# Where the token lists of the later experts come from: one-hot matmuls, or a table in DRAM

## The chip, the cores and the metric

The kernel runs on one core of a Trainium2 chip. The metric is the device time of one execution in microseconds (us); each figure is a median of runs. The core has TensorE (PE in the profile; PEld is its weight load), VectorE (DVE), ScalarE (ACT), GpSimd (POOL) and SyncE (SP), each with an instruction queue of its own, and 16 DMA engines. Engines wait for each other through semaphores only.

## The reference

One layer of a diffusion backbone over T = 384 tokens of width 1024. The first half (adaLN modulation, latent attention, a Conformer convolution) is not touched. The second half is a mixture of experts:

```
scores = sigmoid(t @ router_w)                      # (384, 64)
# 4 of 8 groups, then the best 8 of 64 experts per token; w = their scores, normalised, times 2.5
gates  = sum(one_hot(idx, 64) * w)                  # (384, 64), 8 entries per row are not zero
hid    = silu(t @ exp_w_gate[e]) * (t @ exp_w_up[e]) * gates[:, e]
routed = sum over e of hid @ exp_w_down[e]          # 64 experts, 3 MB of fp32 weights each
x      = x + gate2 * (routed + shared)              # then one final RMSNorm
```

## The kernel before

The instructions of each engine are written out by hand, in the order in which they run; nothing reorders them. After the router, the kernel takes one expert per **step** j: up to 128 tokens of expert j are gathered, sent through its three matrices and scattered. (An expert with over 128 tokens would need more rounds; the number of rounds is read from the data. In the run shown there is one round, 64 steps.) Steps 0 to 7 are unrolled, the middle ones are a hardware loop over blocks of 8 (`in_order`, L462), the last 8 and three to drain are unrolled again.

The **list** of an expert says, for each of 128 slots, which token sits there (`ixt[:, k, 0]`, the row of `h2_d` to gather), which row of `y_d` its result goes to (`ixt[:, k, 1]`, the token times 8 plus the rank of the expert among the token's 8) and with which gate (`gsl[:, k]`). `slot` is the partition that a position has. Before the change each list is made from `pos3` (each token's position in each expert's list, or a large number) and `vals` (token, destination, and the gate in two parts) in three moves:

- DVE `onehot` (L1537) compares `pos3` of one expert with `slot`: a 128x384 tensor of ones and zeros;
- PE `token_list` (L2060): three matmuls of that one-hot with the expert's 4 columns of `vals`, into bank 5;
- DVE `list_of` (L1547) turns the bank into integers `ixt` and the gate `gsl`, and counts up `list_done`.

What each engine does in step k, in order (numbers are experts):

- SP (L642) waits for a raw buffer to be used and loads gate and up weights of k+3, then down weights of k+1. Each load is 1 MB.
- ACT (L1113): silu of k-1, hidden of k-2 (`hidden_hi`), high part of the gate weights of k+1, `rows_out` of k-3 (PSUM to `ys`, two copies, L1110 and L1111), gathered tokens of k+1 (`turn_hi`), high part of the down weights of k-1 (L1078), high part of the up weights of k+1 (L1069).
- DVE (L1634): `hidden` of k-1 (L1599), `hidden_lo`, low part of the gate weights of k+1 (L1455), `list_of` of k+3, `onehot` of k+4, `turn_lo` of k+1 (L1590), low part of the down weights of k-1 (L1584), low part of the up weights of k+1 (L1455 again).
- PE (L2145): `token_list` of k+3, transposes of the tokens of k+1 (L1756), gate and up matmuls of k+1 (24 of 128x512), transposes of the hidden of k-1, then the down matmuls of k-2 (12). Each product is three matmuls (high x high, high x low, low x high), lines L1746 to L1748.
- POOL (L790): `gather` of k+3 (L776), which waits for `list_done`, then `scatter` of k-3 (L785). Both are indirect DMAs.

There are two `ys` buffers. So `rows_out` of k-3 waits until the scatter of k-5, issued two steps before, has landed (L1107).

Of the kernel before, what the change touches and what calls it, by code (L numbers as in the profile page):

```python
# [21 lines left out]
I32 = mybir.dt.int32  # L22
ALU = mybir.AluOpType
# [25 lines left out]
UNROLL = 8  # L49
NO_TOKEN = 4096  # L50


def constants():
# [84 lines left out]
def hybrid_step(nc, x_prompt, x_sample, cache_ckv, cache_krope, c, c_ctx, mod_w, mod_b, norm1_g, w_in,  # L138
# [11 lines left out]
    with ExitStack() as ctx:  # L150
# [124 lines left out]
        token_i = sb("token_i", [P, 1], A + 5.9375, I32)  # L275
        gsl = sb("gsl", [P, UNROLL], R + 8.375)
        sg = sb("sg", [P, FF], R + 9)
        hd = [sb(f"hd{i}", [P, FF], R + 10 + i) for i in range(2)]
# [19 lines left out]
        mod_d = dram("mod_d", [2, 4 * D])  # L298
        y_d = dram("y_d", [T * TOPK, D])

        def conv_slot(k):
# [17 lines left out]
        sinv = cst_of("sin").rearrange("p (t a f) -> p t a f", t=2, a=2)  # L319
        token = cst_of("token")  # L320
        V_G1, V_CB, V_LG, V_LB, V_QG, V_C = 0, 8, 16, 24, 32, 35

# [32 lines left out]
        mod_rows_out, g1_in, a2_in, b2_in = (sem(n) for n in ("mod_rows_out", "g1_in", "a2_in", "b2_in"))  # L355
        x1_done, ssq2_done, r2v, r2a, h2_done = (sem(n) for n in ("x1_done", "ssq2_done", "r2v", "r2a", "h2_done"))
        x1_out = sem("x1_out")
# [368 lines left out]
        def _(pool):  # L726
            pool.memset(zb[:, :, :], 0.0).then_inc(zeros_done, 1)

            pool.wait_ge(latn_done, 2 * NT)
# [50 lines left out]
            def scatter(i, k, last=False):  # L780
# [24 lines left out]
        def _(act):  # L805
# [221 lines left out]
            def mean_square2(t):  # L1027

                act.wait_ge(x1_done, NT + t + 1)
                act.activation(junk2[:, :], x1[:, t, :], ACT.Square, accum_out=stat[:, 40 + t:41 + t]).then_inc(ssq2_done, 1)  # L1030
                act.wait_ge(ssq2_done, t + 1)
                act.activation(stat[:, 44 + t:45 + t], stat[:, 40 + t:41 + t], ACT.Sqrt, scale=1.0 / D,
                               bias=stat[:, 53:54]).then_inc(r2a, 1)

# [132 lines left out]
            for t in range(NT):  # L1167
# [3 lines left out]
                act.activation(tjunk[:, :], acc[:, t, :], ACT.Square, accum_out=stat[:, 16 + t:17 + t]).then_inc(ssq2_done, 1)  # L1171
                act.wait_ge(r2v, t + 1)
                act.activation(stat[:, 60 + t:61 + t], stat[:, 57 + t:58 + t], ACT.Sqrt).then_inc(r2a, 1)


        @block.vector
        def _(dve):
# [254 lines left out]
            def normed2(t):  # L1432

                dve.wait_ge(r2a, t + 1)
                link(dve, "v", dve.reciprocal(stat[:, 48 + t:49 + t], stat[:, 44 + t:45 + t]))
# [111 lines left out]
            def list_of(i, k):  # L1547
                j = i * UNROLL + k
                if isinstance(j, int) and j < 2:
                    p = got(dve, ("list", j))  # L1550
                else:
# [42 lines left out]
            def hidden(i, k):  # L1594
                j = i * UNROLL + k
                dve.wait_ge(sg_done, j + 1)
                if from_step(j, 2):
# [3 lines left out]
                                         op0=ALU.mult, op1=ALU.mult).then_inc(hd_done, 1)  # L1601

            sums = {"all": 0}

# [29 lines left out]
            def step(i, k, left=99):  # L1634
# [31 lines left out]
            turn_lo(0, 0)  # L1666
            shared_hidden(2)
            in_order(dve, step)


# [30 lines left out]
            def normed(t):  # L1701

                dve.wait_ge(ssq2_done, NT + t + 1)
                dve.tensor_scalar(stat[:, 57 + t:58 + t], stat[:, 16 + t:17 + t], 1.0 / D, EPS, ALU.mult, ALU.add).then_inc(r2v, 1)
                dve.wait_ge(r2a, NT + t + 1)
                link(dve, "v", dve.reciprocal(stat[:, 60 + t:61 + t], stat[:, 60 + t:61 + t]))
# [23 lines left out]
        def _(pe):  # L1730
# [500 lines left out]
```

## Time and profile before

| | us |
|---|---|
| median of 3 runs | 1185.79 (1184.06 to 1187.43) |
| the profiled execution's own time | 1187.37 |
| its span, first to last instruction | 1185.6 |
| PE busy, share of the span | 1125.1, 95% |
| DVE busy | 1034.8, 87% |
| ACT busy | 796.4, 67% |
| POOL busy | 235.0, 20% |
| experts' steps | from about 516 to 1145 |

Lines L12 are lines of the kernel. PE's ends are modelled, so its busy share says little; the start of one matmul to the start of the next says more. An idle time is put down to the instruction or DMA that ended it. TensorE's granted clock was 0.98 of full speed over the span.

### The profile page before, as it was taken

The page shows a single profiled execution, that of the slowest core. Times are in us where ns is not written, and L with a number is a line of the kernel's source. Part 1 is how long each engine was busy: PE and PEld are TensorE (multiplying, and loading weights), DVE is VectorE, ACT ScalarE, POOL GpSimd, SP SyncE. Part 2 cuts the span into 40 slices and gives each one's busy share as a digit, 9 for nine tenths or more (in the row PEclk, how much of TensorE's full clock was granted, in tenths as well). Part 3 has the DMA queues.
Part 4 walks back from the last instruction along what each step waited for, and adds up shares of the span by engine and source line. Part 5 has one row for each costly group of instructions (what it writes and reads, how often), then busy time and mean ns, then how long its engine had stood idle before and what let it go on. Part 6 is the DMA issues. An engine that isn't in the chain of part 4 may idle for free.

```text
span 1185.6 us, 16767 instructions
## 1 busy us (share of the span) xinstructions
PE 1125.1 (95%) x5625; PEld 918.9 (78%) x5625; DVE 1034.8 (87%) x1382; ACT 796.4 (67%) x992; POOL 235.0 (20%) x182
## 2 busy tenths in 40 slices
PE   4999999998999999989999999999999999999984
PEld 1799999864557798658888888888888888888851
DVE  4769999989996565869998999999999999999977
ACT  6543232767873632748887888888888888888831
POOL 1000000001123001223422323332323323222210
PEclk8999999998999989999999999999999999999997
DMA  9673446635547227859999999999999999999994
GB/s 349 183 182 107 143 148 171 182 116 173 163 122 235 80 78 274 326 216 343 378 362 356 365 373 369 377 363 346 354 354 365 359 358 380 364 374 365 357 416 178
DMA packets 123259, 329.10 MB, mean 278 GB/s; under 512 B 28248, under 2 KB 69815, under 8 KB 98375
## 3 DMA queue, kind: packets, MB, share of 16 engines
q1 hardware_dynamic: 98656, 290.39, 66.8%
q0 software_dynamic: 21584, 33.79, 8.4%
q10 hardware_dynamic: 2968, 4.26, 1.0%
q8 instruction: 30, 0.49, 0.2%
q14 instruction: 21, 0.17, 0.0%
HBM read 327.70 MB, written 41.66 MB: 312 GB/s over the span
## 4 chain that ended last, share of the span: by engine, by line
PE 75%; DVE 9%; DMA 8%; ACT 5%; issue 2%; SPq 0%; POOL 0%; DVEq 0%; ACTq 0%; POOLq 0%
PE bank L1746 19%; PE bank L1748 19%; PE bank L1747 19%; PE bank L1756 7%; DMA raw<-in_exp_w_down_dram 3%; DVE lgu L1455 2%; DMA y_d<-ys,ixt 2%; PE bank L1941 2%; ACT hi L816 2%; PE bank L1929 1%; DVE lo L1584 1%; PE bank L1762 1%; DMA row1b<-y_d 1%; DMA raw<-in_mod_w_dram 1%; PE bank L1763 1%
## 5 line engine op out<-in xcount | busy, mean ns | idle before, releaser
L1455 DVE TENSOR_TENSOR lgu<-raw,hgu 128x2048 fp32r<-128x2048 f32 x128 | 292.0, 2282 | 1.3 <-ACT hgu L1069 1.3
L1069 ACT ACTIVATE hgu<-raw 128x2048 fp32r<-128x2048 f32 x128 | 245.4, 1917 | 0.4 <-DMA raw<-in_exp_w_gate_dram 0.4
L1746 PE MATMUL bank<-hgu,xgh 128*128 128x512 f32 x512 | 205.8, 402 | 2.4 <-DVE lgu L1455 2.1
L1748 PE MATMUL bank<-hgu,xgl 128*128 128x512 f32 x512 | 200.6, 392 | 0.0
L1747 PE MATMUL bank<-lgu,xgh 128*128 128x512 f32 x512 | 199.2, 389 | 0.0
L1584 DVE TENSOR_TENSOR lo<-raw,hi 128x2048 fp32r<-128x2048 f32 x64 | 147.7, 2308 | 27.8 <-ACT hi L1078 20.1
L1186 DVE TENSOR_TENSOR lo<-raw,hi 128x2048 fp32r<-128x2048 f32 (+2 forms) x57 | 125.8, 2209 | 29.9 <-ACT hi L816 29.9
L776 POOL DMA_INDIRECT xg<-h_d,ixt x64 | 66.3, 1036 | 399.1 <-DVE gsl L1557 372.5
L1078 ACT ACTIVATE hi<-raw 128x2048 fp32r<-128x2048 f32 x64 | 122.9, 1921 | 28.4 <-DMA raw<-in_exp_w_down_dram 28.4
L1284 DVE SCALAR_TENSOR_TENSOR zb<-zb,cwt 128x400 f32<-128x400 f32 x240 | 135.7, 634 | 0.6
L785 POOL DMA_INDIRECT y_d<-ys,ixt x62 | 124.7, 2011 | 48.3 <-ACT ys L1111 28.6
L816 ACT ACTIVATE hi<-raw 128x2048 fp32r<-128x2048 f32 (+2 forms) x57 | 105.1, 1846 | 18.8 <-PE bank L1748 16.0
L1746 PEld LDWEIGHTS bank<-hgu,xgh 128*128 128x128 f32 x512 | 96.2, 188 | 22.2 <-issue 3.2
L1748 PEld LDWEIGHTS bank<-hgu,xgl 128*128 128x128 f32 x512 | 96.1, 188 | 21.3
L1747 PEld LDWEIGHTS bank<-lgu,xgh 128*128 128x128 f32 x512 | 96.4, 188 | 18.5
L1746 PE MATMUL bank<-hi,hdh 128*128 128x512 f32 x256 | 106.4, 416 | 0.3 <-DVE hdl L1631 0.3
L1748 PE MATMUL bank<-hi,hdl 128*128 128x512 f32 x256 | 100.7, 393 | 0.0
L1747 PE MATMUL bank<-lo,hdh 128*128 128x512 f32 x256 | 99.5, 389 | 0.0
L1746 PE MATMUL bank<-hTh,hi 128*128 128x384 f32 x256 | 85.6, 334 | 0.0
L1748 PE MATMUL bank<-hTh,lo 128*128 128x384 f32 x256 | 85.5, 334 | 0.0
L1747 PE MATMUL bank<-hTl,hi 128*128 128x384 f32 x256 | 85.5, 334 | 0.0
L1590 DVE TENSOR_TENSOR xgl<-bank,xgh 128x512 fp32r<-128x512 f32 x128 | 82.0, 682 | 2.7 <-ACT xgh L1086 2.7
(306 smaller groups left out, 2081.0 us busy)
## 6 DMA issues: line engine op xcount, KB each, us to landing
raw<-in_exp_w_gate_dram SPq DMA_DIRECT2D x64, 1024.0 KB
raw<-in_exp_w_up_dram SPq DMA_DIRECT2D x64, 1024.0 KB
raw<-in_exp_w_down_dram SPq DMA_DIRECT2D x64, 1024.0 KB
raw<-in_mod_w_dram SPq DMA_DIRECT2D x20, 1024.0 KB, 5.2
raw<-in_w_in_dram SPq DMA_DIRECT2D x16, 512.0 KB, 5.4
raw<-in_w_in_dram SPq DMA_DIRECT2D x8, 1024.0 KB, 5.4
mraw<-in_mod_w_dram SPq DMA_DIRECT2D x4, 1024.0 KB, 15.7
raw<-in_w_o_attn_dram SPq DMA_DIRECT2D x4, 1024.0 KB, 5.0
```

Source lines behind the costliest of these rows:

```text
L785: pool.indirect_dma_start(y_d, bass.IndirectOffsetOnAxis(ap=ixt[:, k % UNROLL, 1:2], axis=0), (ys_last if last else ys)[k % 2][:, :], None ...
L816: act.activation(hi[place(i)][:, 0:k * w], tile[:, 0:k * w], ACT.Copy).then_inc(hi_done, 1)
L1069: act.activation(hgu[k % 2][:, :, w, :], src, ACT.Copy).then_inc(ghi_done, 1)
L1078: act.activation(hi[down_place(k, last)][:, :], raw[s][:, :], ACT.Copy).then_inc(dhi_done, 1)
L1186: dve.tensor_tensor(lo[place(i)][:, 0:k * w], tile[:, 0:k * w], hi[place(i)][:, 0:k * w].bitcast(F32), ALU.subtract).then_inc(lo_done, 1)
L1284: ins = dve.scalar_tensor_tensor(out=dst, in0=src, scalar=wk, in1=dst, op0=ALU.mult, op1=ALU.add)
L1455: dve.tensor_tensor(lgu[k % 2][:, :, w, :], src, hgu[k % 2][:, :, w, :].bitcast(F32), ALU.subtract).then_inc(glo_done, 1)
L1584: dve.tensor_tensor(lo[to][:, :], raw[s][:, :], hi[to][:, :].bitcast(F32), ALU.subtract).then_inc(dlo_done, 1)
L1746: pe.matmul(out, ah, bh, start=first, stop=False)
L1747: pe.matmul(out, ah, bl, start=False, stop=False)
L1748: return pe.matmul(out, al, bh, start=False, stop=last)
L1756: return pe.transpose(out, src, ident[0:n, 0:n])
```

## The change

Lists 0 to 10 are made as before. The others come from a table in DRAM, `lists_d`, with one row of four words (token, destination, gate, destination) for each of 128 slots of each expert:

- early, POOL fills the table with ones (as integers: an index out of bounds, which an indirect DMA leaves out);
- before step 0, DVE packs position and expert of each token's 8 choices in one key, sorts the keys with `max`, and unpacks them to the table row of each choice (`entry_rows`); in step 0 it picks the 8 gates of each token (`entry_gates`, 24 instructions);
- in steps 0 to 6 POOL writes the entries, 24 indirect DMAs of 128 rows of 16 bytes (`write_lists`); in step 7 it waits for them and reads the table into `listed`;
- from list 11 on, in steps 8 to 60, `token_list` on PE and `onehot` on DVE are gone, and `list_of` is two small copies out of `listed`; it stands at the end of DVE's step, behind the low part of the up weights, and not in its middle.

Two semaphores are merged with older ones (`r2v`, `r2a` with `rms_v`, `rms_a`), with the same order of events.

```diff
+KEY = 2048
+ON_TENSOR = UNROLL + 3
...
+    parts["key"] = np.broadcast_to(KEY * (NE - np.arange(NE))[None, :], (P, NE))
+    parts["dest"] = (TOPK * parts["token"][:, :, None] + np.arange(TOPK)).reshape(P, NT * TOPK)
...
 # gpsimd
             pool.memset(zb[:, :, :], 0.0).then_inc(zeros_done, 1)
+            pool.wait_ge(con_in, 16)
+            pool.dma_start(lists_d.rearrange("(q a) v -> q (a v)", q=P).rearrange("q (b n) -> q b n", n=P),
+                           ones.unsqueeze(1).to_broadcast([P, NJ * 4 // P, P])).then_inc(lists_out, 16)
...
+            def write_lists(first, end):
+                if first == 0:
+                    pool.wait_ge(lists_out, 16)
+                    pool.wait_ge(entry_done, 1)
+                for n in range(first, end):
+                    t, u = n // TOPK, n % TOPK
+                    pool.indirect_dma_start(lists_d, bass.IndirectOffsetOnAxis(ap=entry_row[:, t, u:u + 1], axis=0),
+                                            entry[:, t, u, :], None,
+                                            bounds_check=P * NJ - 1, oob_is_err=False).then_inc(lists_out, 16)
...
                 if from_step(j, 3):
                     scatter(i, k - 3, last=left <= -1)
+                if isinstance(j, int) and j < 7:
+                    write_lists(24 * j // 7, 24 * (j + 1) // 7)
+                if isinstance(j, int) and j == 7:
+                    pool.wait_ge(lists_out, 16 * (NT * TOPK + 1))
+                    pool.dma_start(listed[:, :, :], lists_d.rearrange("(q j) v -> q j v", q=P)).then_inc(lists_out, 16)
...
 # vector: list_of
+                if not isinstance(j, int) or j >= ON_TENSOR:
+                    dve.wait_ge(lists_out, 16 * (NT * TOPK + 2))
+                    dve.tensor_copy(ixt[:, k % UNROLL, :], listed[:, bass.ds(j, 1), 0:2].rearrange("p a v -> p (a v)").bitcast(I32))
+                    dve.tensor_copy(gsl[:, k % UNROLL:k % UNROLL + 1],
+                                    listed[:, bass.ds(j, 1), 2:3].rearrange("p a v -> p (a v)")).then_inc(list_done, 1)
+                    return
...
+            def entry_rows():   # 2 over 128x192, 3 max, then 10 of 128x24
...
+            def entry_gates():
+                for t in range(NT):
+                    for u in range(TOPK):
+                        ins = dve.scalar_tensor_tensor(out=key_gate[:, u, :], in0=keys[:, t, :], scalar=key8[:, t, u:u + 1],
+                                                       in1=rgate[:, t, :], op0=ALU.is_equal, op1=ALU.mult,
+                                                       accum_out=entry[:, t, u, 2:3])
...
+                ins.then_inc(entry_done, 1)
+                dve.wait_ge(entry_done, 1)
...
 # vector: step
-                if left > 3:
+                if isinstance(j, int) and j + 3 < ON_TENSOR:
                     list_of(i, k + 3)
-                if left > 4:
+                if isinstance(j, int) and j + 4 < ON_TENSOR:
                     onehot(i, k + 4)
                 if left > 1:
                     turn_lo(i, k + 1)
+                if isinstance(j, int) and j == 0:
+                    entry_gates()
...
                 if second:
                     down_lo(i, k - 1)
+                if left > 3 and not (isinstance(j, int) and j + 3 < ON_TENSOR):
+                    list_of(i, k + 3)
...
             shared_hidden(2)
+            entry_rows()
             in_order(dve, step)
...
 # tensor: step
-                if left > 3:
+                if isinstance(j, int) and j + 3 < ON_TENSOR:
                     token_list(i, k + 3)
```

On DVE, one step of the hardware loop before the change; `lgu` is the low part of gate or up weights, `lo` that of the down weights, `xgl` that of the gathered tokens, `oh` the one-hot:

```order
L1599 SCALAR_TENSOR_TENSOR hd_176<-bank,gsl,sg 128x256
L1631 TENSOR_TENSOR hdl_181<-bank,hdh_179 128x256
L1455 TENSOR_TENSOR lgu_160<-raw_49,hgu_158 128x8x256
L1556 TENSOR_SCALAR ixt<-bank 128x2
L1557 TENSOR_REDUCE gsl<-bank 128x1
L1544 TENSOR_TENSOR oh_171<-con,pos_129 128x384
L1590 TENSOR_TENSOR xgl_166<-bank,xgh_164 128x512
L1584 TENSOR_TENSOR lo_62<-raw_51,hi_59 128x2048
L1455 TENSOR_TENSOR lgu_160<-raw_50,hgu_158 128x8x256
```

The same step of the changed kernel, where `listed` is the table in SBUF:

```order
L1639 SCALAR_TENSOR_TENSOR hd_186<-bank,gsl,sg 128x256
L1707 TENSOR_TENSOR hdl_191<-bank,hdh_189 128x256
L1489 TENSOR_TENSOR lgu_160<-raw_49,hgu_158 128x8x256
L1630 TENSOR_TENSOR xgl_166<-bank,xgh_164 128x512
L1624 TENSOR_TENSOR lo_62<-raw_51,hi_59 128x2048
L1489 TENSOR_TENSOR lgu_160<-raw_50,hgu_158 128x8x256
L1592 COPY ixt<-listed 128x2
L1593 COPY gsl<-listed 128x1
L1639 SCALAR_TENSOR_TENSOR hd_187<-bank,gsl,sg 128x256
```

The one-hot is gone, and the pair that fills `ixt` and `gsl` has moved from the third place of the step to its end, past four large instructions. On POOL, steps 3 to 7 of the changed kernel, where `lists_d` is the table and `entry` what is written to it:

```order
L794 DMA xg0_162<-h2_d,ixt_172 128x1024
L803 DMA y_d<-ys0_168,ixt_172 3072x1024
L815 DMA lists_d<-entry_176,entry_row_177 24576x4 x3
L794 DMA xg1_163<-h2_d,ixt_172 128x1024
L803 DMA y_d<-ys1_169,ixt_172 3072x1024
L815 DMA lists_d<-entry_176,entry_row_177 24576x4 x4
L794 DMA xg0_162<-h2_d,ixt_172 128x1024
L803 DMA y_d<-ys0_168,ixt_172 3072x1024
L829 DMA listed_175<-lists_d 128x768
```

Three or four writes stand behind each scatter, and in the loop behind these rows gather and scatter alternate as before, the scatter always behind the gather of its step.

## Rows read from the trace of the kernel before

**Rows 1.** The page: busy us, share of the span, instructions.
```profile
PE 1125.1 (95%) x5625; PEld 918.9 (78%) x5625; DVE 1034.8 (87%) x1382; ACT 796.4 (67%) x992; POOL 235.0 (20%) x182
```
**Rows 2.** By stretch: PE, PEld, DVE, ACT, POOL busy us; PE clock, DMA share, GB/s.
```profile
740.00:780.00 40.00, 40.00 (x203) 33.81 (x202) 39.12 (x43) 34.65 (x37) 13.77 (x9) 1.00 0.96 378
...
860.00:900.00 40.00, 40.00 (x204) 33.78 (x203) 38.33 (x43) 34.30 (x38) 12.77 (x9) 1.00 0.94 354
```
**Rows 3.** The chain of work that ended last, 740 to 752: start us, us, what.
```profile
741.97 0.23 PE bank L2072 x3
742.20 0.95 PE bank L1756 x8
...
751.64 0.23 PE bank L2072 x3
```
**Rows 4.** All engines in time, one step: start us, us, what, [idle before].
```profile
742.01 0.60 ACT L1110 ACTIVATE ys<-bank 128x512 f32<-128x512 f32 x1 [0.42 <-PE bank L1748]
...
744.72 1.92 ACT L1078 ACTIVATE hi<-raw 128x2048 fp32r<-128x2048 f32 x1 [0.44 <-DMA raw<-in_exp_w_down_dram]
...
744.88 0.15 DVE L1557 TENSOR_REDUCE gsl<-bank 128x1 f32<-128x2 f32 x1
744.94 0.55 DVE L1544 TENSOR_TENSOR oh<-con,pos 128x384 fp32r<-128x384 f32 x1
...
745.84 1.01 POOL L776 DMA_INDIRECT xg<-h_d,ixt  x1 [5.20 <-DVE gsl L1557]
...
747.16 2.69 POOL L785 DMA_INDIRECT y_d<-ys,ixt  x1 [0.30 <-issue]
...
748.88 2.28 DVE L1455 TENSOR_TENSOR lgu<-raw,hgu 128x2048 fp32r<-128x2048 f32 x1
```
**Rows 5.** ACT in time, two steps later.
```profile
761.42 0.60 ACT L1110 ACTIVATE ys<-bank 128x512 f32<-128x512 f32 x1 [0.61 <-PE bank L1748]
```
**Rows 6.** Who waited for whom: us in total, times, longest us.
```profile
ACT hi L1078 <- DMA raw<-in_exp_w_down_dram: 28.4, 19, 4.0
...
ACT ys L1110 <- PE bank L1748: 26.4, 50, 0.9
```
**Rows 7.** Instructions of line L785, the scatters.
```profile
L785 POOL DMA_INDIRECT y_d<-ys,ixt x62: 961/1014/4836, 551.9 to 1138.4; - x62
...
DMA to landing us min/median/max: 7.0/7.1/7.2
```
**Rows 8.** Line L762, two early gathers of 128 rows.
```profile
DMA to landing us min/median/max: 10.1/10.5/11.0
```
**Rows 9.** The chain of work that ended last, 480 to 640.
```profile
561.09 15.30 DMA y_d<-ys,ixt
```
**Rows 10.** DVE in time, around steps 0 and 1.
```profile
522.70 0.16 DVE L1556 TENSOR_SCALAR ixt<-bank 128x2 int32<-128x2 f32 x1 [2.64 <-PE bank L2072]
...
527.34 0.48 DVE L1599 SCALAR_TENSOR_TENSOR hd<-bank,gsl,sg 128x256 f32<-128x256 f32 x1 [1.77 <-ACT sg L1094]
529.14 2.29 DVE L1455 TENSOR_TENSOR lgu<-raw,hgu 128x2048 fp32r<-128x2048 f32 x1 [1.31 <-ACT hgu L1069]
```
**Rows 11.** DVE in time, the router.
```profile
499.48 0.18 DVE L1496 TENSOR_SCALAR rgm<-rgm 128x24 f32<-128x24 f32 x1
...
500.08 0.48 DVE L1502 MAX8 rk<-rsel 128x8 f32<-128x64 f32 x3
...
506.23 0.89 DVE L1532 SCALAR_TENSOR_TENSOR pos<-bank,rtmp 128x192 f32<-128x192 f32 x3
```
**Rows 12.** The page: costliest groups: busy us, mean ns, idle before.
```profile
L785 POOL DMA_INDIRECT y_d<-ys,ixt x62 | 124.7, 2011 | 48.3 <-ACT ys L1111 28.6 <-issue 19.8
```
**Rows 13.** Who waited for whom, 505 to 605: us in total, times, longest.
```profile
POOL xg L776 <- DVE gsl L1557: 48.8, 8, 8.4
```
**Rows 14.** POOL in time, step 4.
```profile
559.78 1.01 POOL L776 DMA_INDIRECT xg<-h_d,ixt  x1 [3.01 <-DVE gsl L1557]
561.09 4.80 POOL L785 DMA_INDIRECT y_d<-ys,ixt  x1 [0.30 <-issue]
```

More of the change, by code:

```diff
@@ L276, in hybrid_step @@
         gsl = sb("gsl", [P, UNROLL], R + 8.375)
+        listed = sb("listed", [P, NJ, 4], R)
+        entry = sb("entry", [P, NT, TOPK, 4], A + 7.25)
+        entry_row = sb("entry_row", [P, NT, TOPK], A + 7.625, I32)
+        keys = sb("keys", [P, NT, NE], R + 14)
+        key_gate = sb("key_gate", [P, 8, NE], R + 12)
+        key8 = sb("key8", [P, NT, TOPK], R + 15)
+        key_i, key_p, key_q, key_r = (sb(f"key_{n}", [P, NT, TOPK], R + 15.125 + 0.125 * i, I32)
+                                      for i, n in enumerate("ipqr"))
         sg = sb("sg", [P, FF], R + 9)
@@ L355, in hybrid_step @@
         mod_rows_out, g1_in, a2_in, b2_in = (sem(n) for n in ("mod_rows_out", "g1_in", "a2_in", "b2_in"))
-        x1_done, ssq2_done, r2v, r2a, h2_done = (sem(n) for n in ("x1_done", "ssq2_done", "r2v", "r2a", "h2_done"))
+        x1_done, ssq2_done, h2_done = (sem(n) for n in ("x1_done", "ssq2_done", "h2_done"))
+        entry_done, lists_out = sem("entry_done"), sem("lists_out")
         x1_out = sem("x1_out")
@@ L1171, in _ @@
                 act.activation(tjunk[:, :], acc[:, t, :], ACT.Square, accum_out=stat[:, 16 + t:17 + t]).then_inc(ssq2_done, 1)
[L1172 to L1173 removed]
+                act.wait_ge(rms_v, t + 3)
+                act.activation(stat[:, 60 + t:61 + t], stat[:, 57 + t:58 + t], ACT.Sqrt).then_inc(rms_a, 1)
         @block.vector
@@ L1550, in list_of @@
                     p = got(dve, ("list", j))
-                else:
+                elif isinstance(j, int) and j < ON_TENSOR:
                     dve.wait_ge(list_filled, j - 1)
@@ L1601, in hidden @@
                                          op0=ALU.mult, op1=ALU.mult).then_inc(hd_done, 1)
+            def entry_rows():
+                first = pos3[:, :, 0:NE]
+                link(dve, "v", dve.scalar_tensor_tensor(out=keys[:, :, :], in0=first, scalar=512.0,
+                                                        in1=key_of.unsqueeze(1).to_broadcast([P, NT, NE]),
+                                                        op0=ALU.is_lt, op1=ALU.mult))
+                link(dve, "v", dve.tensor_tensor(keys[:, :, :], keys[:, :, :], first, ALU.add))
+                for t in range(NT):
+                    ins = dve.max(key8[:, t, :], keys[:, t, :])
+                dve.tensor_copy(entry[:, :, :, 0].bitcast(I32), token.unsqueeze(2).to_broadcast([P, NT, TOPK]))
+                for v in (1, 3):
+                    dve.tensor_copy(entry[:, :, :, v].bitcast(I32), dest)
+                link(dve, "v", ins)
+                link(dve, "v", dve.tensor_copy(key_i[:, :, :], key8[:, :, :]))
+                dve.tensor_scalar(key_p[:, :, :], key_i[:, :, :], 7, 4, ALU.bitwise_and, ALU.logical_shift_left)
+                dve.tensor_scalar(key_r[:, :, :], key_i[:, :, :], 1, NE * 3, ALU.logical_shift_right, ALU.bitwise_and)
+                link(dve, "v", dve.tensor_scalar(key_q[:, :, :], key_i[:, :, :], 3, 15, ALU.logical_shift_right, ALU.bitwise_and))
+                link(dve, "v", dve.tensor_tensor(key_p[:, :, :], key_p[:, :, :], key_q[:, :, :], ALU.add))
+                dve.tensor_scalar(key_q[:, :, :], key_i[:, :, :], 11, None, ALU.logical_shift_right)
+                link(dve, "v", dve.scalar_tensor_tensor(out=key_p[:, :, :], in0=key_p[:, :, :], scalar=float(NJ),
+                                                        in1=key_r[:, :, :], op0=ALU.mult, op1=ALU.add))
+                dve.scalar_tensor_tensor(out=entry_row[:, :, :], in0=key_p[:, :, :], scalar=float(NE),
+                                         in1=key_q[:, :, :], op0=ALU.add, op1=ALU.subtract)
@@ new lines, in entry_gates @@
+            def entry_gates():
+                for t in range(NT):
+                    for u in range(TOPK):
+                        ins = dve.scalar_tensor_tensor(out=key_gate[:, u, :], in0=keys[:, t, :], scalar=key8[:, t, u:u + 1],
+                                                       in1=rgate[:, t, :], op0=ALU.is_equal, op1=ALU.mult,
+                                                       accum_out=entry[:, t, u, 2:3])
+                    if t < NT - 1:
+                        link(dve, "v", ins)
+                ins.then_inc(entry_done, 1)
+                dve.wait_ge(entry_done, 1)
```

10 lines of the change are left out of this document (6 added, 4 removed).

## The prediction, made before the changed kernel was run

> **What bounds the kernel now.** I read the page's busy line first, then the experts' part by stretches, then the chain of waits inside one step, then who waits for whom. The page puts PE at 95% and DVE at 87% [rows 1], but these are means. In the experts' part PE is never idle, its clock is granted in full, DVE is busy for 38 to 39 of 40 us, ACT for 34, and the DMA engines for 0.94 to 0.96 of the time [rows 2]. So three resources are within a few per cent of each other, and a saving on one of them is worth only what the next one leaves.
>
> The chain inside a step is PE alone, with matmuls starting every 0.23 us. From one list's matmuls to the next list's it is 751.64 - 741.97 = 9.67 us [rows 3]; from one `rows_out` on ACT to that two steps later it is 761.42 - 742.01 = 19.41 us, 9.70 each [rows 4, 5]. I use 9.70 as the pace. That the DMA engines are nearly as tight shows on ACT, which waited 19 times, 28.4 us in all, for down weights [rows 6].
>
> **What is taken away.** Lists 11 to 63 are 53, handled in steps 8 to 60.
> - PE: three small matmuls per list hold the chain for 0.23 us [rows 3]. 53 x 0.23 = 12.2 us, all of it on the path as long as PE sets the pace.
> - DVE: the one-hot takes 0.55 us [rows 4], and two small instructions of 0.15 us become two small copies, which I price the same. DVE gets 0.5 us per step of room. It lies beside PE's work and is worth nothing by itself.
>
> With only this, the pace would be 9.70 - 0.23 = 9.47 us.
>
> **What is moved, and what it makes late.** This is the term that decides. `list_of` goes to the end of DVE's step. POOL's queue is in order: in each step the gather of k+3 waits for the list, and the scatter of k-3 stands behind that gather. The scatter itself needs nothing of the list; it is late because of its place. Step by step, with the rows of one step [rows 4]:
> - Before: the list is ready at 744.88 + 0.15 = 745.03, the gather starts at 745.84 (0.81 later), the scatter at 747.16 (1.32 later). Two steps later ACT's `rows_out`, at 761.42 [rows 5], needs this scatter landed, as it writes the same `ys`. The landing may take 761.42 - 747.16 = 14.3 us.
> - After, at the same pace: the low part of the up weights ends at 748.88 + 2.28 = 751.16; plus 0.2 for the two copies, 0.81 and 1.32, the scatter starts at 753.5. The landing may take 7.9 us.
>
> If it takes longer, it is a loop and not a one-time delay. `rows_out` stands on ACT ahead of `turn_hi`, the down weights and the up weights, and DVE's low part of the up weights, behind which the list now stands, follows these. From `rows_out` to the end of that DVE instruction it is 751.16 - 742.01 = 9.15 us, of which 0.44 is a wait for the down load [rows 4], so 8.7. The loop closes over two steps: 8.7 + 0.2 + 0.81 + 1.32 + L = 11.0 + L, with L the time from a scatter's start on POOL to its landing. PE's 9.47 us holds if L is under 7.9; each us of L beyond costs half a us per step, 26 us over 53 steps.
>
> **What L is.** The trace shows it directly only in places. With the DMA engines nearly free at the end it was 7.0 to 7.2 us [rows 7]. In step 4 it was 15.3, with 4.8 of them on POOL [rows 9, 14]. In between ACT waited for PE and not for a scatter in 50 steps [rows 6], so it was mostly under 14.3. Nearest in kind are two indirect gathers of 128 rows of 4 KB on the same queue beside other traffic: 10.1 to 11.0 [rows 8]. A scatter moves 3072 / 64 = 48 rows on average, not 128, which makes it shorter; the expert weights keep the DMA engines busier than they were then, which makes it longer. And if the pace falls to about 10 us, the same bytes leave the engines at 0.95 x 9.70 / 10.0 = 0.92 and the landing gets shorter again. I take 9.1 us. Then two steps take 20.1 us, one 10.05, and 53 x (10.05 - 9.70) = +18.5 us. The ends: at 7.0 the loop needs 9.0 us and does not bind, so -12 us; at 10.5 it is 10.75 and +56 us; at 14.3, 12.65 and +156 us, which would need the worst landing in each step.
>
> The Trainium skill, "DMA: Bandwidth & Descriptors", section on the anatomy of one DMA on the SWDGE path, fits a GpSimd DMA as 2.0 us plus bytes over 436 GB/s, by which 48 rows would land in about 2.5 us and this wait would never bind. The trace disagrees, 7.0 us at least.
>
> **The gather** is later as well: it starts at 752.2, and PE turns its rows two steps after the 742.20 of rows 3, at 761.6. So it may take 9.4 us, a little more than the scatter has. It is issued before the scatter and stands ahead of it on the queue, so I cost it at nothing; if it took the 10.5 of rows 8, it would be the scatter's rival for the same loop.
>
> **The start.** `entry_rows` is 2 instructions over 192 columns at 0.30 (0.89 for 3), three `max` at 0.16 (0.48 for 3) and ten small ones at up to 0.18 [rows 11]: about 2.8 us, in front of a `list_of` before which DVE stood idle for 2.64 us [rows 10]: +0.2. `entry_gates` is 24 instructions over 64 columns. The trace has none with an accumulator; between `max` over 64 at 0.16 and the 0.30 of 192 columns I take 0.16, for the width: 3.9 us (7.2 at the other end), into idle times of 1.77 + 1.31 us [rows 10]: +0.8 (+4.1). Together +1.
>
> POOL gets 24 writes. The price of one there is between 1.01 us, the median, and 4.84, the longest [rows 7]; I take 1.01, as most indirect DMAs do, plus 0.31 to the next. 3 or 4 per step are 4.5 us, where POOL, with scatters of 4.8 us, stood idle for only 3.0 us before the gather of step 4 [rows 14]: 1.5 us late per step over four steps, on scatters that in this stretch already took 15.3. Half of these 6 us I count: +3. At the scatters' mean of 2.0 [rows 12], 24 x 2.3 = 55 us would have to fit in POOL's idle time, 48.8 us between 505 and 605 [rows 13], of which I leave out some 6 before the entries are ready: 43, so +12. At 4.84 it would be +80. The fill and the reading of the table move 0.4 MB each, in an early stretch and inside one step, about 1 us of the rate of rows 2: hidden, unless the reading is not there by the end of step 8.
>
> The Trainium skill, same page, rules for kernel authors, says that transfers under 64 KB are mostly overhead and should be joined. A write here carries 2 KB. No row shows the cost of such a write; it is the rule that speaks for the POOL rival below.
>
> **The sum.** +18.5 (the 12.2 of PE is inside it, since the loop and not PE sets the pace) + 1 + 3 = +22.5, on the profiled execution's 1187.4: 1209.9. The median of the runs lies 1.6 lower: 1208.3, say 1208.
>
> **The rivals.**
> - *The matmuls' time is given back.* L stays under about 8 us, PE goes on setting the pace: -12.2 + 4 = -8, about 1178. For it: the last scatters landed in 7.0 to 7.2. Against: DMA is at 0.95, and at 9.47 us the same bytes would ask for 0.97. This is the side opposite to the forecast.
> - *DMA takes over.* L does not bind, but neither can the loads come faster: pace 9.6 to 9.7, so -5 to 0, + 4 at the start: 1185 to 1190. For it: the 28.4 us of waits for down weights.
> - *POOL is jammed at the start.* The loop does not bind, but the 24 writes cost 2 us or more each: +12 to +40, 1198 to 1226.
> - That lists come out wrong or are not used would not change the time and is not weighed.
>
> **How the numbers follow.** Forecast 0.62, of its own between 1193 and 1250; PE's time given back 0.16; DMA 0.12; POOL's jam 0.10. A measurement of this kernel can tell about 0.3%, 3.6 us, from no change. Faster: 0.16. Same: 0.08 of the DMA case. Slower: 0.62 + 0.10 + 0.04 = 0.76. The range reaches from the first rival's 1178 to 1245, which is L of about 10: nearly 0.1 is left out on either side.
>
> **What would show it.** Right: ACT's `ys` waits for the DMA to `y_d` in most steps from 11 on; PE has idle time; the pace is about 10 us; the DMA share falls to 0.92; DVE has more idle time. The start: POOL's writes last about 1 us each. Wrong: ACT's `ys` still waits for PE, and the lists' 0.23 us are gone from PE's chain with a pace of 9.5 (first rival), or ACT's waits for weights have grown (second).

## The result and the profile after

| | us | ratio to before, 95% interval |
|---|---|---|
| before, beside it on the same chip | 1184.94 | |
| changed kernel, median of 4 | 1292.56 (1279.51 to 1375.03) | 1.0804 [1.0786, 1.0822] |
| predicted | 1208 (1178 to 1245) | |

Slower, as forecast, but by four times as much. Two of the four runs were disturbed; the ratio leaves them out, and by it the changed kernel takes 1280.2 us. The profiled execution took 1281.86, its span is 1280.0. Below, each kernel is placed by its ratio: +8.04% is the changed kernel, and 1% is 11.85 us.

The page's busy line answers to [rows 1]. PE's and DVE's busy times hardly changed; they are a smaller share of a longer span. POOL has 94 us more.

```profile
PE 1137.9 (89%) x5466; PEld 912.8 (71%) x5466; DVE 1022.1 (80%) x1393; ACT 788.4 (62%) x992; POOL 329.3 (26%) x208
```

By stretch, as [rows 2] (the columns are the same): PE is idle for 4 to 5 of 40 us, DVE for 6 to 10, and the DMA share fell from 0.96 and 0.94 to 0.86 and 0.80. Nothing is full any more; something waits in a circle.

```profile
740.00:780.00 40.00, 34.77 (x163) 28.54 (x164) 30.04 (x32) 26.45 (x32) 15.95 (x8) 0.96 0.86 321
860.00:900.00 40.00, 35.95 (x170) 29.42 (x169) 33.55 (x34) 28.93 (x34) 13.49 (x7) 0.96 0.80 297
```

The page's groups name the circle (line, engine, op, out<-in, count | busy us, mean ns | idle before and who ended it). ACT's `rows_out`, which had waited for PE [rows 6], waits for the scatter to `y_d`, and PE's transposes wait for the gather of `xg`:

```profile
L1837 PE MATMUL bank<-con,xg 128*128 128x128 f32 x512 | 72.5, 287 | 76.8 <-DMA xg<-h_d,ixt 76.0
L1144 ACT ACTIVATE ys<-bank 128x512 f32<-128x512 f32 x62 | 37.2, 600 | 163.6 <-DMA y_d<-ys,ixt 161.5
L1112 ACT ACTIVATE hi<-raw 128x2048 fp32r<-128x2048 f32 x64 | 124.1, 1938 | 6.6 <-DMA raw<-in_exp_w_down_dram 6.6
```

One loop over two steps in time, to be held against [rows 4, 5] (ACT, DVE and POOL, each by its own timeline):

```profile
743.28 0.60 ACT L1144 ACTIVATE ys<-bank 128x512 f32<-128x512 f32 x1 [3.85 <-DMA y_d<-ys,ixt]
...
754.50 0.60 ACT L1144 ACTIVATE ys<-bank 128x512 f32<-128x512 f32 x1 [3.20 <-DMA y_d<-ys,ixt]
...
765.97 0.60 ACT L1144 ACTIVATE ys<-bank 128x512 f32<-128x512 f32 x1 [3.45 <-DMA y_d<-ys,ixt]
```
```profile
749.39 2.28 DVE L1489 TENSOR_TENSOR lgu<-raw,hgu 128x2048 fp32r<-128x2048 f32 x1
751.59 0.16 DVE L1592 COPY ixt<-listed 128x2 int32 x1
751.66 0.15 DVE L1593 COPY gsl<-listed 128x1 f32 x1
...
752.45 2.28 DVE L1489 TENSOR_TENSOR lgu<-raw,hgu 128x2048 fp32r<-128x2048 f32 x1
```
```profile
752.64 2.98 POOL L794 DMA_INDIRECT xg<-h_d,ixt  x1 [7.59 <-issue]
755.93 1.01 POOL L803 DMA_INDIRECT y_d<-ys,ixt  x1 [0.30 <-issue]
```

From `rows_out` to the end of the up weights' low part 751.67 - 743.28 = 8.39 us (predicted 8.7); from there to the scatter's start 755.93 - 751.67 = 4.26 (predicted 2.33); from there to the `rows_out` that it releases 765.97 - 755.93 = 10.04 (predicted 9.1). Sum 22.69 us for two steps, 11.35 each. This loop is one of the longer ones: over 43 such waits between 600 and 1140 us the last part was 6.5 to 11.8 us, 9.6 on the median. The mean over steps 8 to 60, from one `hidden` on DVE to the next, is 11.08 us against 9.70 before: 52 x 1.38 = 72 us. At the start `hidden` of step 8 came 17.1 us later than before, at the end 3 us are added: 92 of the 94.4 us between the two spans.

### The profile page after: what moved, and what is told of

Its sections match the earlier page's. It is cut to its first block, busy times and chain, and to the rows that moved or that the text cites. A ratio compares the mean times of both kernels' runs of the same rounds, so it can differ in the third digit from the quotient of the medians.

```text
span 1280.0 us, 16321 instructions
## 1 busy us (share of the span) xinstructions
PE 1137.9 (89%) x5466; PEld 912.8 (71%) x5466; DVE 1022.1 (80%) x1393; ACT 788.4 (62%) x992; POOL 329.3 (26%) x208
## 4 chain that ended last, share of the span: by engine, by line
DMA 36%; issue 5%; ACT 4%; PE 4%; DVE 1%; ACTq 0%; POOL 0%; POOLq 0%; DVEq 0%; SPq 0%
DMA y_d<-ys,ixt 32%; DMA xg<-h_d,ixt 2%; ACT xgh L1120 2%; ACT ys L1145 1%; DMA row1b<-y_d 1%; PE bank L1827 1%; PE bank L1828 1%; PE bank L1829 1%; PE bank L2280 1%; DMA listed<-lists_d 1%; ACT hi L1112 1%; PE bank L1837 0%; DVE lgu L1489 0%; DVE lo L1624 0%; ACT ys L1144 0%
## 5 line engine op out<-in xcount | busy, mean ns | idle before, releaser
L794 POOL DMA_INDIRECT xg<-h_d,ixt x64 | 160.7, 2511 | 390.1 <-issue 326.7
L1827 PE MATMUL bank<-hgu,xgh 128*128 128x512 f32 x512 | 211.8, 414 | 3.3 <-DVE lgu L1489 3.0
L1829 PE MATMUL bank<-hgu,xgl 128*128 128x512 f32 x512 | 205.3, 401 | 0.0
L1828 PE MATMUL bank<-lgu,xgh 128*128 128x512 f32 x512 | 205.3, 401 | 0.0
L1837 PE MATMUL bank<-con,xg 128*128 128x128 f32 x512 | 72.5, 287 | 76.8 <-DMA xg<-h_d,ixt 76.0
L1144 ACT ACTIVATE ys<-bank 128x512 f32<-128x512 f32 x62 | 37.2, 600 | 163.6 <-DMA y_d<-ys,ixt 161.5
L1837 PEld LDWEIGHTS bank<-con,xg 128*128 128x128 f32 x512 | 58.4, 145 | 96.7 <-issue 88.7
L1827 PEld LDWEIGHTS bank<-hgu,xgh 128*128 128x128 f32 x512 | 100.3, 196 | 24.3 <-issue 3.9
L1828 PEld LDWEIGHTS bank<-lgu,xgh 128*128 128x128 f32 x512 | 100.1, 195 | 19.3
L803 POOL DMA_INDIRECT y_d<-ys,ixt x62 | 79.9, 1288 | 41.6 <-ACT ys L1145 23.2
```

What stands on the lines that cost most here:

```text
L794: pool.indirect_dma_start(xg[k % 2][:, :], None, h2_d, bass.IndirectOffsetOnAxis(ap=ixt[:, k % UNROLL, 0:1], axis=0), bounds_check=T - 1, ...
L1827: pe.matmul(out, ah, bh, start=first, stop=False)
L1828: pe.matmul(out, ah, bl, start=False, stop=False)
L1829: return pe.matmul(out, al, bh, start=False, stop=last)
L1837: return pe.transpose(out, src, ident[0:n, 0:n])
```

## The experiments

Fourteen kernels were run, in four batches, each beside the kernel before (1186.64, 1184.47, 1185.02 and 1185.44 us in them). "Pace" is us per step from step 8 to 60 in the profiled execution; kernels 4 and 14, whose steps do the work of before in this stretch, have 9.73 and 9.67 against its 9.70, so a difference of 0.03 says nothing.

| kernel | us | ratio, interval | pace |
|---|---|---|---|
| changed kernel | 1292.56 (1280.2 by the ratio) | 1.0804 [1.0786, 1.0822] | 11.08 |
| 1 list in mid-step | 1232.06 | 1.0375 [1.0358, 1.0393] | 10.05 |
| 2 scatter first | 1241.86 | 1.0456 [1.0431, 1.0482] | 10.46 |
| 3 before, late gather | 1246.76 | 1.0504 [1.0460, 1.0548] | 10.83 |
| 4 table not used | 1199.95 | 1.0105 [1.0086, 1.0123] | 9.73 |
| 5 list ahead of up | 1265.27 | 1.0674 [1.0652, 1.0697] | 10.71 |
| 6 list ahead of down | 1232.15 | 1.0396 [1.0379, 1.0413] | 10.02 |
| 7 as 1, matmuls kept | 1233.05 | 1.0412 [1.0386, 1.0438] | 10.08 |
| 8 as 1, one-hot kept | 1234.63 | 1.0422 [1.0404, 1.0439] | 10.07 |
| 9 rows spread | 1262.59 | 1.0648 [1.0627, 1.0669] | 10.81 |
| 10 as 1, rows spread | 1200.17 | 1.0129 [1.0112, 1.0146] | 9.48 |
| 11 before, rows bunched | 1213.05 | 1.0254 [1.0227, 1.0281] | 10.09 |
| 12 DVE waits for POOL | 1305.37 | 1.1023 [1.0981, 1.1065] | 11.50 |
| 13 as 10, later switch | 1188.55 | 1.0029 [1.0015, 1.0042] | 9.58 |
| 14 DVE's start alone | 1187.73 | 1.0025 [1.0010, 1.0040] | 9.67 |

### 1. The list back in the middle of the step

```diff
-                if isinstance(j, int) and j + 3 < ON_TENSOR:
+                if left > 3:
                     list_of(i, k + 3)
...
-                if left > 3 and not (isinstance(j, int) and j + 3 < ON_TENSOR):
-                    list_of(i, k + 3)
```

> The changed kernel with the two list copies put back to the middle of DVE's step, where the list was made before; table, writes and everything else stay. Theory (the late list holds up the scatter behind the gather, 1.38 us per step): the pace goes from 11.08 back to 9.5 to 9.7 us, ACT's ys waits for PE again and not for the DMA to y_d, and what is left against the kernel before is the start (+17 us up to step 8) less up to 12 us of PE's list matmuls: 1185 to 1203 us. Rival (the pace is lost to the table itself, or to TensorE's clock and idle time, wherever the copies stand): 1270 us or more, pace 11.

1232.06 us. The waits for `y_d` are gone, so the place of the list was a cause, worth 8.04 - 3.75 = 4.3 points, 51 us. But the pace stopped at 10.05, above the 9.70 of a kernel with more work. Who waited, from 700 to 1150:

```profile
ACT hi L1112 <- DMA raw<-in_exp_w_down_dram: 92.8, 45, 2.9
```

Before, this wait was 28.4 us in the whole run [rows 6]. Neither theory had it. Experiments 7 and 8 ask why.

### 2. The scatter ahead of the gather

```diff
+                late = not isinstance(j, int)
+                if late:
+                    scatter(i, k - 3, last=left <= -1)
                 if left > 3:
                     gather(i, k + 3)
-                if from_step(j, 3):
+                if from_step(j, 3) and not late:
                     scatter(i, k - 3, last=left <= -1)
```

> The changed kernel, but in steps from 8 on POOL issues the scatter ahead of the gather, so it no longer stands behind the late list. Theory A (only the scatter's place matters): pace 9.5 to 9.7 us, 1190 to 1205 us. Theory B (the late gather would bind next: after, PE waited 76 us for xg; 0.9 us from the list to the gather, 11.5 to its landing, 1.1 on PE, 7.4 on ACT and DVE, 20.9 us for two steps): pace about 10.4 us, 1184 + 17 + 52 x 0.7 = 1237, between 1220 and 1245 us, with ACT's ys free of DMA waits and PE waiting for xg.

1241.86 us, pace 10.46, as theory B had it. No wait for `y_d` is left among the longest, and PE waits for `xg` in its place (620 to 1160): the late gather is a second loop just behind the first.

```profile
PE bank L1840 <- DMA xg<-h_d,ixt: 47.7, 29, 4.7
```

### 3. The kernel before, with a gather that is late

```diff
+                if not isinstance(j, int):
+                    pool.wait_ge(glo_done, up_lo)     # up_lo = 2 * j - 2
```

> The kernel before, lists from one-hot matmuls, with one wait more: from step 8 on the gather also waits until DVE has finished the low part of the up weights, the place where the changed kernel makes its list. No table, no writes. Theory (the lateness alone makes the loss): pace about 11.1 us, 1184 + 52 x 1.38 = 1256, between 1245 and 1265 us, and gathers of 3 us on POOL. Rival (the table or the missing matmuls play a part in the loop): under 1235 us.

1246.76 us. With no table, no writes and no copies, ACT waits for the scatter again (620 to 1160):

```profile
ACT ys L1112 <- DMA y_d<-ys,ixt: 117.4, 47, 4.2
```

The lateness alone makes 5.0 of the 8.0 points. The time came out at the low end of the theory's range, with a pace of 10.83 and not 11.1; the gathers took 2.65 us on the mean from 700 to 1150 (3 forecast). What the loop of the changed kernel loses beyond this goes with where the rows lie: kernel 9 below is the changed kernel with its rows placed as in this one, and runs at 10.81.

### 4. The table built, read in part and not used

> The changed kernel's keys, 24 gates, 24 table writes and the reading of the table (a third of it, 128 experts' rows, to another place in SBUF), but all 64 lists come from the one-hot matmuls as before, so the table isn't used. Shows the cost of the start by itself. Theory: the writes fill POOL's queue in steps 1 to 7, +14 to +20 us and the old pace of 9.70 after: 1198 to 1204 us. Rival (the start's loss of 17 us is mostly the wait for the table's reading and for late lists): +5 to +10 us, 1189 to 1194 us.

Only a third of the table is read, into free memory; all lists come from one-hots. 1199.95 us: in the profiled execution step 11 is 14.3 us late, and every step after it between 12.7 and 14.6. That is the start by itself, as the theory had it (1198 to 1204).

### 5 and 6. The list one and two places earlier

In 5 `list_of` stands between the low parts of the down and the up weights, in 6 ahead of both.

> The changed kernel with the two copies of the list one place earlier in DVE's step, ahead of the second low part of the up weights instead of behind it. Theory A (a POOL indirect DMA that begins while a DVE instruction over 128x2048 in SBUF runs lasts until 0.9 us after its end): the gather starts inside that DVE instruction and lasts 3.0 us, so the scatter starts some 1.2 us after the end of the DVE instruction, not 2.3 us earlier as the copies do; pace (8.4 + 1.2 + 10.4) / 2 = 10.0 us, 1230 to 1240 us. Theory B (only the place of the list counts, the gather costs 1.0 us): gathers of 1.0 us, scatter starts 2.2 us earlier than by A, the scatter's loop is (8.4 - 1.0 + 10.4) / 2 = 8.9 and no longer binds; ACT waits for down weights as in the kernel with the list in the middle of the step, 1232 us.

> As the kernel before it, with the copies one more place earlier, ahead of the low part of the down weights: 2.2 us earlier again. Theory A: the gather starts inside the low part of the down weights and is held through the low part of the up weights as well, so it lasts about 5 us and the scatter starts where it does in the kernel before it; the same time within 0.5%, 1230 to 1240 us. Theory B: gathers of 1.0 us and a scatter another 2.2 us earlier.

1265.27 and 1232.15 us. One DVE instruction of 2.3 us between the two places makes 33 us. In 5, DVE and POOL in time:

```profile
811.97 2.28 DVE L1489 TENSOR_TENSOR lgu<-raw,hgu 128x2048 fp32r<-128x2048 f32 x1
...
814.89 2.28 DVE L1489 TENSOR_TENSOR lgu<-raw,hgu 128x2048 fp32r<-128x2048 f32 x1
```
```profile
812.88 2.26 POOL L794 DMA_INDIRECT xg<-h_d,ixt  x1 [6.01 <-issue]
815.45 2.61 POOL L803 DMA_INDIRECT y_d<-ys,ixt  x1 [0.30 <-issue]
```

The gather began under one such DVE instruction and ended at 815.14, 0.89 us after its end (814.25); the scatter began under the next and ended at 818.06, 0.89 us after 817.17. Theory A had the gather held and overlooked the scatter, so the time lies outside both theories (1230 to 1240, and 1232). In 6 DVE waits for ACT just behind the copies, up to 3.0 us, and 25 of the 44 gathers that start between 700 and 1150 slip through that gap at 1.0 us; the others are held for 2.3 to 4.5 us (theory A had about 5 in every step). The time is that of kernel 1 and its 10.05: inside theory A's range, but not by its mechanism, since the scatter did not start where it does in 5.

### 7 and 8. What holds kernel 1 at 10.05: its faster PE, or its freer DVE?

7 runs three list matmuls per step again, on old one-hots; 8 runs the one-hots again; nothing reads either.

> The kernel with the list in the middle of DVE's step, and three small matmuls per list again on PE in every step (on old one-hots; nothing reads their result). Theory A (in that kernel PE ran at 9.35 us per step from step 10 to 15, faster than the DMA engines bring the weights; the down loads fell behind and stay late at 10.05): PE holds 9.65 to 9.70 again, the down waits nearly vanish, and only the 24 us of the start remain: 1205 to 1212 us. Theory B (the 10.05 comes from something else: the table, the step with the long wait, the DVE room): no change, 1232 us.

> The kernel with the list in the middle of DVE's step, and the one-hot of 0.55 us again on DVE in every step (nothing reads it from the twelfth list on). Theory A: PE is still without its three matmuls and outruns the loads: 10.0 to 10.1 us per step, 1232 us. Theory B (DVE's room is what moves the loads out of step): pace 9.7, 1205 to 1212 us.

1233.05 and 1234.63 us: neither. My theory A of 7 fell: with PE back at its old work the down loads are as late. In 8 theory B fell; that the time is the one of its theory A does not speak for it, as 7 had refuted the same mechanism. What was left was the list itself. Read side by side, the two ways of making it differ in one rule, which partition gets place p of an expert's list (`slot` holds the place of each partition i; the arrow gives it the other way round):

```
constants():    "slot": i % 8 * 16 + i // 8          -> partition 8 * (p mod 16) + p / 16
entry_rows():   key_p = (key & 7) << 4, + (key >> 3) & 15  -> partition 16 * (p mod 8) + p / 8
```

For the mean list of 48 rows the first rule fills 3 of every 8 partitions, the second 6 of every 16 and none of the other 10.

### 9 to 11. Rows spread and rows bunched

```diff
-    key_p = tensor_scalar(key_i, 7, 4, bitwise_and, logical_shift_left)
+    key_p = tensor_scalar(key_i, 15, 3, bitwise_and, logical_shift_left)
-    key_q = tensor_scalar(key_i, 3, 15, logical_shift_right, bitwise_and)
+    key_q = tensor_scalar(key_i, 4, 7, logical_shift_right, bitwise_and)
```

Kernel 9 is the changed kernel with this, 10 is kernel 1 with this, and 11 is the kernel before with the table's rule in its constant (`i % 16 * 8 + i // 16`) and nothing else.

> The changed kernel with one thing more: the table puts the token at place p of an expert's list on partition 8 * (p mod 16) + p / 16, as the one-hots do, and not on 16 * (p mod 8) + p / 8. By the table's rule the mean list of 48 rows lies on the first 6 of every 16 partitions, by the one-hots' on 3 of every 8. Theory A (a DMA engine serves 8 neighbouring partitions, so by the table's rule 8 of 16 engines move all rows of gathers and scatters): in the changed kernel the 8 busy engines have 384 / 16 x 0.336 + 96 / 8 x 0.166 = 10.06 us of packets per step and the others 8.06, with this change all have 9.06; rows land 1 to 2 us earlier, and the loop of two steps is shorter by that: 1245 to 1275 us. Theory B (the place of the rows does not matter, the landing is what it is): 1292 us.

> The kernel with the list in the middle of DVE's step, and rows spread over the partitions as in the kernel before it. Theory A (its 10.05 us per step were the 10.06 us of packets of the 8 busy engines): the down waits go, the pace is 9.35 (PE alone) to 9.65, and with the start's 17 to 24 us the time is 1185 to 1206 us. Theory B (the 10.05 come from elsewhere): 1232 us.

> The kernel before, with nothing changed but the constant that gives a place in the list its partition: 16 * (p mod 8) + p / 8, the table's rule. No table. Theory A: the packets of the 8 busy engines ask for 10.06 us per step, ACT waits for down weights in most steps, pace 10.0 to 10.1, 1201 to 1212 us. Theory B: 1186 us, no change.

9 and 10 came out inside theory A's ranges, 11 one us above its (pace 10.09, as forecast). So where the rows lie costs time. Kernel 11 shows it most plainly, since it has the same instructions, packets and bytes as before and is 2.54% slower. From 700 to 1150, first before, then 11, then 10 (columns as in [rows 2]):

```profile
700.00:1150.00 450.00, 449.62 (x2244) 376.15 (x2243) 425.18 (x451) 373.88 (x414) 134.55 (x90) 1.00 0.95 367
```
```profile
700.00:1150.00 450.00, 438.05 (x2176) 364.46 (x2176) 410.39 (x438) 360.61 (x403) 106.42 (x88) 1.00 0.91 348
```
```profile
700.00:1150.00 450.00, 445.50 (x2171) 369.87 (x2170) 412.77 (x421) 380.00 (x425) 159.93 (x92) 1.00 0.96 371
```

And who waited in the same stretch, first before, then in 11 and in 10:

```profile
ACT hi L1078 <- DMA raw<-in_exp_w_down_dram: 10.3, 7, 4.0
```
```profile
ACT hi L1078 <- DMA raw<-in_exp_w_down_dram: 89.6, 45, 2.7
```
```profile
ACT hi L1112 <- DMA raw<-in_exp_w_down_dram: 40.4, 25, 5.9
```

In 11 ACT waits for weights while the DMA engines are on the mean busy for only 0.91. Both fit if some engines are full and others not. But which ones is not as my theory A had it (one engine for 8 neighbouring partitions). No view names the engine of a packet, yet the packed trace has the start of every one, and the last two scatters, of 34 and 53 rows, run beside a light stream in which an engine begins a row of 4 KB every 0.31 us:

| rows of 4 KB begun per 0.311 us | scatter of 34 rows | scatter of 53 rows, first to last |
|---|---|---|
| before (rows spread) | 8, 9, 2, 8, 7 | 2.03 us |
| 11 (rows bunched) | 7, 4, 4, 5, 4, 4, 4, 2 | 2.45 us |
| changed kernel (bunched) | 5, 4, 4, 4, 4, 5, 4, 4 | 2.39 us |

In 11 the 34 rows fall into four series of 8 rows, each 0.31 us behind the last, and two single rows. One engine for 8 neighbours would make 8 engines of 4 or 5 rows there, and 16 engines before: some 16 starts per 0.311 us, and the 53 rows, at most 4 to an engine, all begun within about 1.2 us. What fits is an engine for two groups of 4 partitions, 32 apart. Then the rule of before already puts the mean list of 48 rows on 8 engines, 6 rows each, and the table's rule puts 8 rows on each of four engines and 4 on each of four others; the remaining 8 have none in either case.

Of a step's 384 weight packets each of the 16 engines has 24. By the median durations from 700 to 1100, 0.309 us for a weight packet of 8 KB and 0.159 for a row, the fullest engines have 24 x 0.309 + 12 x 0.159 = 9.3 us of packets per step before, and 24 x 0.309 + 16 x 0.159 = 10.0 with the rows bunched. That is an estimate. Kernels 1, 6, 7, 8 and 11 have paces of 10.02 to 10.09, the kernel before 9.70 and kernel 10 9.48. The 10.06 of theory A rests on the mean durations (0.336 and 0.166) and on 12 bunched rows per step where the four fullest engines carry 16. The means ask for too much (they would put before at 10.05, and it runs at 9.70), the 12 rows for too little, and the two cancel: that 10.06 was met is luck. Its forecast of landings 1 to 2 us earlier in 9 did not come: 9.3 us on the median of 40 against 9.6. Neither rule uses all 16 engines for the rows; one that does was not run.

### 12. DVE holds back until POOL is through

```diff
+                if from_step(j, 3):
+                    pool.memset(mark[:, :], 0.0).then_inc(zeros_done, 1)      # POOL, behind the scatter
...
+                if left > 1 and not isinstance(j, int):
+                    dve.wait_ge(zeros_done, j - 2)                            # DVE, ahead of gate_up_lo(k + 1, 0)
```

(Each scatter waits for the memset before it, which is long done.)

> The changed kernel, and DVE's first low part of the up weights in each step from the ninth on waits until POOL is through with the gather and the scatter that the list of the step before released (POOL counts with a memset of one column behind its scatter). Theory A (a POOL indirect DMA that begins while a DVE instruction over 128x2048 in SBUF runs lasts until 0.9 us after its end): gathers fall from 3.0 to 1.0 us, the scatter starts 2 us earlier in each step, the loop over two steps is 2 us shorter, up to 52 us in all, less what DVE's wait makes late: 1245 to 1275 us, though DVE has a wait more. Theory B (the 3.0 us are not DVE's doing): gathers stay at 3.0 us, and with the wait added the time is 1292 us or above.

1305.37 us, slower still and on theory B's side in time, and yet the gathers did what theory A says (700 to 1150, columns as the page's groups):

```profile
L795 POOL DMA_INDIRECT xg<-h_d,ixt x39 | 39.7, 1017 | 354.1 <-issue 289.6 <-ACT ys L1149 64.5
```

1017 ns on the mean, against 2982 for the median of the changed kernel's 64. The time was lost to the wait itself:

```profile
DVE lgu L1493 <- POOL mark L828: 107.1, 39, 3.8
```

DVE's own work from this instruction to the end of `hidden_lo` is 8.7 us, and 2.7 us of wait for POOL follow each time: a loop of one step, 11.4 us, where two steps had closed in 22.7. The hold of 2 us is shown; what it costs the changed kernel in time is not measured by itself.

### 13 and 14. The start

14 keeps only DVE's keys and gates. 13 is kernel 10 with `step(1, k)` written out for k = 0 to 7 (the table serves from list 19 on), two writes per step in steps 0 to 11, and the table read in step 12, into a place that is free only as the load of `final_g` moves behind ACT's steps.

> The kernel with the list in the middle of DVE's step and rows spread over the partitions (1200 us), and three things more: steps 8 to 15 are written out as steps 0 to 7 are, so that the lists up to 18 come from one-hots and the first from the table is list 19, in step 16; the 24 writes go two per step into steps 0 to 11; the table is read in step 12, into a tile of its own, so four steps lie between the reading and its first use. Theory A (of the start, the 11.7 us at step 8 are the wait for the reading, and the writes' rest comes from crowding): 45 x 0.2 = 9 to 12 us of the loop gained as before, less 2 for the eight lists, the start +4 to +8: 1179 to 1188 us, about the kernel before. Theory B (the stall only moves to step 16, or eight more steps written out cost something themselves): 1196 to 1206 us.

> The kernel in which the table is built but every list comes from the one-hots (1200 us), without the 24 writes and without the reading: only the DVE work on keys and gates stays, and nothing reads it. Theory A (DVE's part costs the 3.7 us that are left at step 2, POOL's writes the other 10): 1188 to 1192 us. Theory B (DVE's work at the start sets off the rest, by putting the first steps out of time): 1196 to 1201 us.

DVE's part costs 0.25%, 3 us. The other 10 or so of kernel 4 are POOL's part: the writes, its wait for them and the reading, which 14 leaves out together. In the changed kernel the 24 writes took (ns, shortest/median/longest):

```profile
L815 POOL DMA_INDIRECT lists_d<-entry,entry_row x24: 968/1004/4587, 531.2 to 603.6; - x24
```

Eleven of them took 1.9 to 4.6 us and the mean is 1.81. The reading (POOL, then DVE in time) stands behind all of them:

```profile
609.35 0.61 POOL L829 DMA_DIRECT2D listed<-lists_d  x1
621.60 3.04 POOL L794 DMA_INDIRECT xg<-h_d,ixt  x1 [11.64 <-issue]
```
```profile
620.47 0.17 DVE L1592 COPY ixt<-listed 128x2 int32 x1 [3.47 <-DMA listed<-lists_d]
```

13 came to 1188.55 us, 0.3% above before (0.15 to 0.42) and just above theory A's 1188: its gain in the loop (9.58 against 9.70, 6 us) does not quite pay for the rest. It is the best of the versions that read their lists from the table, and no better than the kernel before.

## Why the prediction was wrong, step by step

Of the 72 us by which 1208 was short of 1280, the loop has about 54 (11.08 us per step against 10.05), the start 13 and the end 3.

- **The list moves late and a loop of two steps closes: right.** ACT's `ys` waits for `y_d` 56 times, PE has idle time, DVE too. By kernels 9 and 10, which differ in this alone, it costs 6.48 - 1.29 = 5.2 points, 62 us.
- **"The scatter starts at 753.5", with the gather ahead of it at 0.81 + 1.32: wrong.** The gather took 2.98 us, not 1.01, because DVE starts its next 128x2048 subtraction 0.2 us before it. The row was there: the scatter of [rows 4] took 2.69 us and [rows 12] had a mean of 2011 against the usual 1014. I took the scatters' long times for a property of scatters. This term failed most: it was mis-sized by 1.93 us of a loop of 22.7. That DVE holds POOL is shown (kernel 12); how much of the time it makes is not, since kernel 12 paid for it with another wait.
- **L = 9.1: too small**, 10.04 in this loop and 9.6 on the median. My relief ("the same bytes leave the engines at 0.92 and the landing gets shorter") did not come, though the mean share fell to 0.84. The four fullest engines were, by the estimate above, still at 10.0 / 11.08 = 0.90, but that is not the whole of it: with the rows spread (kernel 9) it was still 9.3. What else sets the landing stays open.
- **The gather cost at nothing: wrong.** I named the rival in one sentence and gave it no price. PE waited 76.0 us for `xg`, and with the scatter out of its way (kernel 2) the gather's loop alone holds 10.46.
- **Rows bunched: missing altogether.** I wrote that wrong or unused lists would not matter and never asked whether they are the same lists. They hold the same tokens on other partitions, and so less evenly over the DMA engines. That is 1.6 points in the changed kernel, 2.5 once the list is early, and 2.5 in the kernel before.
- **The start, +4: measured +17.** The gates were 24 x 0.21 = 5.1 us instead of 3.9. POOL's writes took 1.0 us on the median as I had it, but 1.81 on the mean, since those that began under one of DVE's long subtractions were held: nearer to the scatters' 2.0 of [rows 12], which I had priced at +12 and given to a rival. From 531 to 610 POOL had no idle time but 0.3 us between two instructions, where I had let half of 1.5 us per step count: `hidden` of steps 4 to 7 came 3.6, 5.4, 5.6 and 14.5 us late. And the reading of the table, which I had called hidden unless it came too late, came too late.
- **PE's 0.23 us per list: right, and small.** Kernel 10 runs at 9.48 against 9.70, until the down loads stop it.

In points: 4.3 for the list's place (kernel 1), 2.5 for the rows (kernel 10), 1.3 for start less PE's gain: 8.0. In the other order the rows come first with 1.6 and the list's place has 5.2. The direction came out right by the mechanism that was forecast, the loop through `y_d`; its size did not.

## What to carry to other kernels

When a change makes the same data by another way, compare where each element lands, not only what it is: a partition also decides the DMA engine, and here a list that puts 8 rows on its fullest engines where it had put 6 cost 2.5% at equal bytes, while the mean DMA share went down. A wait for DMA beside a mean share well under full is the sign of it. And an instruction that is moved behind a long DVE instruction takes its followers on in-order queues with it, so each of them needs its own loop worked out, with the duration it has in its new surroundings.

## What the runs showed of the hardware that I had not expected

- An indirect DMA on POOL that starts while a DVE subtraction of two SBUF tiles of 128x2048 runs lasts until about 0.9 us after that instruction's end (2.26, 2.61, 2.98 and up to 3.04 us). In the traces of all sixteen kernels 1041 start so: 920 end 0.83 to 0.96 us behind it, 51 that much behind the next such instruction (up to 5.3 us in all), and 70, all begun within 0.05 us of the subtraction's own start, are not held. Of the 1327 others, 1308 took 1.0 to 1.1 us. The Trainium skill, "SBUF — State Buffer", section "SBUF: two separate sides", has VectorE hold a port pair that it shares with GpSimd for the whole of an instruction, in a 2-port perf mode or, against a GpSimd instruction that reads SBUF, with two SBUF inputs; its example of a DMA that is held up is of the first kind. The trace agrees with the second kind if an indirect DMA, which takes its row numbers from `ixt` in SBUF, counts as one that reads SBUF; no run here separates that.
- Bunching 48 of 128 rows on 6 of every 16 partitions costs 2.54% at equal bytes (kernel 11). The Trainium skill, "DMA: Bandwidth & Descriptors", section "The descriptor swizzle", has an engine serve two groups of 4 partitions 32 apart in a full copy of 128. The trace agrees, for scatters that leave rows out as well: by it the 34 rows of the last scatter but one lie as 8, 8, 8, 8, 1 and 1 on six engines, which is what the packets of kernel 11 show. For the gathers, which engine moves a row was not read from the trace.
- A direct DMA of 0.4 MB took 10.9 us from its issue to landing in the middle of the weights' traffic, more than a step.
